# Gate and up of the 32 sample rows computed for two feed-forward steps at once, and the first down-projection operands requested earlier

## The reference

```python
def swiglu(h, w_gate, w_up, w_down):
    return (jax.nn.silu(h @ w_gate) * (h @ w_up)) @ w_down

yp = yp + swiglu(rms_norm(yp, g_ffn[l]), w_gate[l], w_up[l], w_down[l])
ys = ys + swiglu(rms_norm(ys, g_ffn[l]), w_gate[l], w_up[l], w_down[l])
```

## Time and profile before

| | |
|---|---|
| median of 3 runs | 1041.6 us (1041.6 to 1042.43) |
| the profiled execution | 1042.83 us, of which span 1041.1 us |
| PE busy | 1011.4 us, 97% of the span |
| DVE, ACT, POOL busy | 618.8, 390.7, 401.2 us |
| granted TensorE clock, mean | 0.994 of full |

### The profile page before, as it was taken

The page is one execution under the profiler, slowest core; times in us unless marked ns, Lnnn a source line. Parts: engine busy times, 40 slices in busy tenths (PEclk is TensorE's granted clock), DMA queues, the critical chain, the costliest instruction groups (busy, mean ns, idle before and its releaser), DMA issues.

```text
span 1041.1 us, 16425 instructions
## 1 busy us (share of the span) xinstructions
PE 1011.4 (97%) x5754; PEld 836.1 (80%) x5754; DVE 618.8 (59%) x918; ACT 390.7 (38%) x720; POOL 401.2 (39%) x445
## 2 busy tenths in 40 slices
PE   5999999999999999999999999999998999999996
PEld 4999998888887887887788787778877777877785
DVE  6375637756355686675575667666663737535725
ACT  6411245454232443333333333333333446334431
POOL 2010100000000457687696686776872300202055
PEclk9999999999999999999999999999999999999998
DMA  8311331101222444364554643643636999478814
GB/s 281 96 44 43 83 85 42 42 2 41 102 86 82 127 139 145 113 182 130 154 157 120 188 143 112 192 146 107 201 107 205 302 344 388 161 287 298 304 41 166
DMA packets 166658, 155.84 MB, mean 150 GB/s; under 512 B 16400, under 2 KB 129808, under 8 KB 166608
## 3 DMA queue, kind: packets, MB, share of 16 engines
q1 hardware_dynamic: 166608, 155.16, 46.4%
HBM read 114.17 MB, written 41.06 MB: 149 GB/s over the span
## 4 chain that ended last, share of the span: by engine, by line
PE 85%; DMA 6%; DVE 6%; ACT 1%; SPq 1%; issue 1%; POOL 1%; POOLq 0%; ACTq 0%; DVEq 0%
PE ps L1089 26%; PE ps L1090 25%; PE ps L1091 25%; DMA xd_in<-act_scratch 4%; PE ps L1371 2%; PE ps L1126 2%; DMA act_scratch<-act_sums 1%; PE ps L1261 1%; PE ps L1239 1%; DVE x_dn L1865 1%; DMA out_state_gmlp_v_sample<-work 1%; PE ps L1223 1%; DVE work L1950 1%; PE ps L1461 1%; DVE ln_st L1944 1%
## 5 line engine op out<-in xcount | busy, mean ns | idle before, releaser
L1089 PE MATMUL ps<-x_forms,w_forms 128*128 128x512 f32 (+1 forms) x644 | 248.4, 386 | 3.5 <-DVE w_forms L1865 2.5
L1090 PE MATMUL ps<-x_forms,w_forms 128*128 128x512 f32 (+1 forms) x644 | 245.9, 382 | 0.0
L1091 PE MATMUL ps<-x_forms,w_forms 128*128 128x512 f32 (+1 forms) x644 | 245.4, 381 | 0.0
L1089 PEld LDWEIGHTS ps<-x_forms,w_forms 128*128 128x128 f32 x644 | 121.8, 189 | 35.6 <-issue 8.3
L1091 PEld LDWEIGHTS ps<-x_forms,w_forms 128*128 128x128 f32 x644 | 121.8, 189 | 23.5
L1090 PEld LDWEIGHTS ps<-x_forms,w_forms 128*128 128x128 f32 x644 | 121.8, 189 | 22.3
L1089 PE MATMUL ps<-w_dn,x_dn 128*128 128x512 f32 x308 | 122.2, 397 | 3.3 <-DVE x_dn L1865 2.7
L1091 PE MATMUL ps<-w_dn,x_dn 128*128 128x512 f32 x308 | 120.7, 392 | 0.0
L1090 PE MATMUL ps<-w_dn,x_dn 128*128 128x512 f32 x308 | 120.5, 391 | 0.0
L941 POOL TENSOR_SCALAR meansq<-sumsq 128x1 f32<-128x1 f32 (+1 forms) x27 | 10.4, 385 | 255.0 <-ACT xn_ffn L1509 226.4
L1668 ACT CAST w_forms<-w_sums 128x512 fp32r<-128x512 f32 x88 | 54.6, 623 | 115.5 <-PE ps L1091 115.5
(11 more groups left out here) (246 smaller groups left out, 2094.4 us busy)
## 6 DMA issues: line engine op xcount, KB each, us to landing
xd_in<-act_scratch SPq DMA_DIRECT2D x35, 512.0 KB, 7.5
t_raw<-in_w_down SPq DMA_DIRECT2D x88, 128.0 KB, 2.6
act_scratch<-act_sums SPq DMA_DIRECT2D x22, 512.0 KB, 4.7
y_acc_odd<-in_w_down SPq DMA_DIRECT2D x22, 512.0 KB, 6.1
wd_in<-t_scratch SPq DMA_DIRECT2D x20, 512.0 KB, 7.5
wd_in<-in_w_down SPq DMA_DIRECT2D x15, 512.0 KB, 7.1
stage<-in_w_in SPq DMA_DIRECT2D x28, 256.0 KB, 3.7
w_stage_even<-in_w_gate SPq DMA_DIRECT2D x22, 256.0 KB, 3.4
```

The costliest lines, as they stand in the source:

```text
L1089: mm(out, wh, xh, start=first, stop=False, skip_group_check=onto)
L1090: mm(out, wh, xl, start=False, stop=False, skip_group_check=onto)
L1091: return mm(out, wl, xh, start=False, stop=last, skip_group_check=onto)
```

## The change

First, `sample_step(c, q)` becomes `sample_pair(c)`: the eight matmuls of both steps of a chunk stand together, after P2 of the second step of the chunk before, in one bank (columns 0 to 255 for the first step, 256 to 511 for the second). Copy, additions, SiLU, product and store each handle both halves at once, and are executed 11 times instead of 22. In the first step the pair stands after the first half `j = 0`. The waits follow: P6 waits for `sample_summed` only where `q == 1`, and `sample_pair` waits for the weights of both steps.

Second, SP asks for the first two weight operands of the down projection (`load_w(0)`, `load_w(1)`) before `store_step` of step 20, and for the first two activation operands before the last two pieces of down-weight sums. ACT and DVE take the first weight operand before `copy_p57` and `p5_p7` of the last step, and the first activation operand right behind them.

```diff
-            def store_sample(c, q):
-                sp.wait_ge(sample_hidden, 2 * c + (q + 1))
-                sp.dma_start(sample_scratch.ap()[:, bass.ds(2 * P * c + P * q, P)],
-                             sample_h[q][:, :]).then_inc(sample_out[q], 16)
+            def store_sample(c):
+
+                sp.wait_ge(sample_hidden, c + 1)
+                sp.dma_start(sample_scratch.ap()[:, bass.ds(2 * P * c, 2 * P)].rearrange("p (q t) -> p q t", q=2),
+                             sample_h[:, :, :]).then_inc(sample_out, 16)
...
             last = STEPS - 1
+            load_piece(CHUNKS - 1, 0)
+            store_sums(CHUNKS - 2)
+            store_piece(CHUNKS - 1, 0)
+            load_piece(CHUNKS - 1, 1)
+            store_piece(CHUNKS - 1, 1)
+            load_piece(CHUNKS - 1, 2)
             for i in range(2):
                 sp.wait_ge(y_spilled[i], 16 * len(range(i, ROWS, 2)))
+            load_w(0)
+            load_w(1)
+            store_step(CHUNKS - 1, 0)
+            load_x(0)
+            load_x(1)
+            store_piece(CHUNKS - 1, 2)
+            load_piece(CHUNKS - 1, 3)
             sp.wait_ge(hidden_out[0], 16 * CHUNKS)
-            for k in range(GROUPS_A_FORM):
+            for k in range(2, GROUPS_A_FORM):
                 load_w(k)
                 load_x(k)
...
-            def sample_step(c, q):
-
-                s = 2 * c + q
-                pe.wait_ge(w_landed[q], 64 * c + 64)
-                pe.wait_ge(u2_ready, s + 1)
-                if isinstance(s, int) and s == 0:
+            def sample_pair(c):
+
+                for q in range(2):
+                    pe.wait_ge(w_landed[q], 64 * c + 64)
+                pe.wait_ge(u2_ready, 2 * c + 1)
+                if isinstance(c, int) and c == 0:
                     pe.wait_ge(x_sample_ready, 1)
-                for k in range(KT):
-                    t = mm(ps[QUARTERS[k % 4], BANK_6[q], 0:2 * P].rearrange("p (h c) -> p h c", h=2),
-                           x_sample[:, k, :], w_stage[q][:, :, k, :], start=k < 4, stop=k >= KT - 4)
+                for q in range(2):
+                    for k in range(KT):
+                        out = ps[QUARTERS[k % 4], BANK_6[0], 2 * P * q:2 * P * q + 2 * P].rearrange("p (h c) -> p h c", h=2)
+                        t = mm(out, x_sample[:, k, :], w_stage[q][:, :, k, :], start=k < 4, stop=k >= KT - 4)
                 t.then_inc(sample_fed, 1)
...
             def ffn_step(c, q, more=True):
                 for p in range(PRODUCTS):
-                    product(2 * c + q, q, p)
-                    if p == P2 and more:
-                        sample_step(*((c, 1) if q == 0 else (c + 1, 0)))
+                    product(c, q, p)
+                    if p == P2 and q == 1 and more:
+                        sample_pair(c + 1)
...
             last = STEPS - 1
             copy_p1(last, 1)
+            down_weight_hi(0)
             copy_p57(last, 1)
-            form_hi(0, 0)
+            act_hi(0)
             silu_c11(last, 1)
...
             second_u(last, 1)
+            down_weight_lo(0)
             p5_p7(last, 1)
-            for g in range(3):
+            act_lo(0)
+            for g in range(1, 3):
                 form_lo(0, g)
```

More of the change, by code:

```diff
@@ L360, in build @@
         x_sample = place("x_sample", [P, KT, DEC], h_at + 63488)
-        sample_gu = [place(f"sample_gu{x}", [DEC, 2 * P], h_at + 64512 + 1024 * x) for x in range(2)]
-        sample_h = [place(f"sample_h{x}", [DEC, P], h_at + 66560 + 512 * x) for x in range(2)]
+        sample_gu = place("sample_gu", [DEC, 2, 2, P], h_at + 64512)
+        sample_h = place("sample_h", [DEC, 2, P], h_at + 66560)
         w_stage = [place("w_stage_even", [P, 2, KT, P], wbuf_at), place("w_stage_odd", [P, 2, KT, P], wbuf_at + 16384)]
@@ L509, in build @@
         sample_hidden = sem("sample_hidden")
-        sample_out = [sem(f"sample_out{x}") for x in range(2)]
+        sample_out = sem("sample_out")
         act_sum_1 = sem("act_sum_1")
@@ L791, in store_piece, with ffn_pair @@
                              t_out[x % 2][:, :, :]).then_inc(t_stored[x % 2], 16)
-            def ffn_pair(c, more):
-                if more:
-                    next_weights(2 * c, 0)
+            def ffn_pair(c):
+                next_weights(2 * c, 0)
                 load_piece(c, 0)
@@ L801, in ffn_pair @@
                 load_piece(c, 1)
-                if more:
-                    next_weights(2 * c + 1, 1)
+                next_weights(2 * c + 1, 1)
                 store_piece(c, 1)
@@ L806, in ffn_pair @@
                 if isinstance(c, int) and c == 0:
-                    store_sample(0, 0)
+                    store_sample(0)
                 store_step(c, 0)
-                store_sample(c, 1)
                 store_piece(c, 2)
                 load_piece(c, 3)
[L813 to L816, removed]
+                store_step(c, 1)
+                store_sample(c + 1)
+                store_piece(c, 3)
+            ffn_pair(0)
             with sp.Fori(1, CHUNKS - 1) as c:
[L818 to L822, removed]
+                ffn_pair(c)
             def load_w(k):
@@ L877, in _ @@
                 if k == 2:
-                    for x in range(2):
-                        sp.wait_ge(sample_out[x], 16 * CHUNKS)
+                    sp.wait_ge(sample_out, 16 * CHUNKS)
                     for x in range(4):
@@ L1702, in silu_c12, with first_quarter, silu_sample @@
                 nc.scalar.activation(cc[q][:, 1, cols], cc[q][:, 1, cols], ACT.Silu).then_inc(c12_silu, 1)
-            def first_quarter(c, q):
-                s = 2 * c + q
-                act.wait_ge(sample_fed, s + 1)
-                if not isinstance(s, int) or s >= 2:
-                    act.wait_ge(sample_hidden, s - 1)
-                nc.scalar.copy(sample_gu[q][:, :], ps[QUARTERS[0], BANK_6[q], 0:2 * P]).then_inc(sample_first, 1)
-            def silu_sample(c, q):
-                act.wait_ge(sample_summed, 2 * c + (q + 1))
-                nc.scalar.activation(sample_gu[q][:, 0:P], sample_gu[q][:, 0:P], ACT.Silu).then_inc(sample_silu, 1)
+            def first_quarter(c):
+                act.wait_ge(sample_fed, c + 1)
+                if not isinstance(c, int) or c >= 1:
+                    act.wait_ge(sample_hidden, c)
+                nc.scalar.copy(sample_gu[:, :, :, :].rearrange("p q h t -> p (q h t)"), ps[QUARTERS[0], BANK_6[0], :]
+                               ).then_inc(sample_first, 1)
+            def silu_sample(c):
+                act.wait_ge(sample_summed, c + 1)
+                nc.scalar.activation(sample_gu[:, :, 0, :], sample_gu[:, :, 0, :], ACT.Silu).then_inc(sample_silu, 1)
             for i in range(ROWS):
@@ L1749, in _ @@
             weight_hi(0, 1, 2)
-            silu_sample(0, 0)
+            silu_sample(0)
             copy_p57(0, 0, 1)
@@ L1756, in _ @@
             silu_c12(0, 0, 1)
-            first_quarter(0, 1)
             weight_hi(0, 1, 6)
-            silu_sample(0, 1)
             def ffn_step(c, q):
@@ L1774, in ffn_step @@
                 weight_hi(*following, 6)
-                silu_sample(*following)
+                if q == 1:
+                    silu_sample(c + 1)
             ffn_step(0, 1)
@@ L2279, in ffn_step @@
                 hidden(s, q)
-                hidden_sample(*following)
+                if q == 1:
+                    hidden_sample(c + 1)
             ffn_step(0, 1)
```

51 lines of the change are left out of this document (25 added, 26 removed).

## The result

The changed kernel takes **1035.24 us** (median of 4 runs, 1034.6 to 1036.26) against 1041.6 us: ratio 0.9939, 95% interval 0.9927 to 0.9951, 6.4 us less. A second comparison (`e8_after_again`) gave 0.9924 (0.9909 to 0.9939), 7.1 us less. The forecast was 1032.7 us, its range 1031.5 to 1036.5. The median is above the 1031.5 to 1034.2 us that the prediction gave to its own sum; it is inside the range because that reached on to partial forms of the rivals. The profiled execution took 1034.63 us where that of before took 1042.83 us, so the two traces differ by 8.2 us and the medians by 6.4: the execution of before was 1.2 us over its median and this one 0.6 us under. Nothing was predicted of the part before 348 us, and its end moved by 0.1 us between these two traces (first P1 at 350.97 and 350.88 us).

What follows compares the result with a forecast made beforehand. PE was taken to bound the feed-forward loop, with the DMA queue nearly full where the down projection begins. 3.6 + 1.0 + 3.8 + 0.5 = 8.9 us off the median 1041.6 gave 1032.7 us, range 1031.5 to 1036.5.

Steps and rivals of the forecast that it cites:

- Part 1: Pairs in the steady steps: one passage into and out of small tiles saved per pair, ten pairs, 3.6 us (2.8 to 4.0).
- I take 0.36: Passage saved per steady pair, in us, chosen from 0.28 to 0.40 because only the first wave took 0.24.
- Part 2: First pair: 1.24 us leaves the first step's end, extra work fills PE's wait, 0.2 us stall; 1.0 us (0.7 to 1.2).
- Part 3: Start of the down projection: wait 2.73 plus low clock 1.5 less a P3 stall of 0.4, 3.8 us (3.0 to 4.3).
- landing at 795.2: First weight load of the down projection lands midway between 794.25 and 796.05 us, so P3 stalls 0.4 us.
- The copy waits long: Rival at the last P3: `wd_in(0)` takes 7.4 us, P3 stalls 3.2 us, the clock falls; 1037.0 us, chance 0.12.
- an outcome without a stall: Before the last P3: followers take nothing from `wd_in(0)`, landing nearer 3.6 us, no stall, sum 0.4 us larger.
- The clock term: Start of the down projection: without the 2.73 us wait PE's clock doesn't fall, nine starts take 1.5 us less.
- Part 4: Sample additions in the down projection: queue gains about 5 us against PE's 3.8, the 0.6 us wait goes; 0.5 us (-3.8 to 0.6).
- ready some 5 us earlier: Third activation operand of the down projection, now behind two loads instead of in a queue of six; `blocks` and `hidden` follow.
- given back at the sample additions: Rival: the queue's chain doesn't move, PE waits 4.4 us there, parts 3 and 4 give nothing; 1037.0 us, chance 0.10.
- signs of being wrong: A PE wait over 1.5 us at P3 or the sample additions, or two steps still taking 40.6 us.

Runs made afterwards that it cites:

- e8_after_again: The changed kernel, unaltered, timed and traced a second time: 1034.26 us, 0.9924 of the kernel before.
- e7: The changed kernel with the pair's two halves apart, after P7 and after P2 of the same step, evacuated together: 1037.87 us, 0.9969 of the kernel before.
- e6: The changed kernel with only the first weight operand requested early; the second and both activation operands behind the last down-weight sums: 1037.68 us, 0.9963 of the kernel before.
- e3: The changed kernel with `copy_p57` ahead of the first weight cast on ACT and `p5_p7` ahead of the subtraction on DVE: 1033.61 us, 0.9921 of the kernel before.
- e1: The changed kernel with the tail of SP, ACT and DVE as before, so the pair alone: 1037.59 us, 0.9959 of the kernel before.
- f4: The kernel before, unaltered, run once more for a second trace: 1041.94 us in its one execution.
- e2: The kernel before with the changed tail of SP, ACT and DVE, so the early requests alone: 1039.24 us, 0.9975 of the kernel before.
- g2: The kernel of e3 run again: 1034.38 us, 0.9936 of the kernel before.
- f1: The changed kernel with the last step's `blocks`, `hidden` and SiLU ahead of the third operands on DVE and ACT: 1036.17 us, 0.9951 of the kernel before.
- g1: The kernel of f2 with SP's last store behind the fifth pair of loads and last sums ahead of two raw loads: 1031.17 us, 0.9901 of the kernel before.
- f2: The kernel of e3 with the last step's `blocks`, `hidden` and SiLU ahead of the third operands: 1035.99 us, 0.9944 of the kernel before.
- e4: The kernel of e3 with DVE's first sample additions two groups of operands earlier in its list: 1032.88 us, 0.9912 of the kernel before.

## Why the prediction was right, and where not

**Part 1 was right, its size too small.** The passage is there and belongs to the change of tiles, as e7 shows. The step that was mis-sized is "I take 0.36" from the starts of the waves: it measured 40.61 - 40.17 = 0.44 us a pair, 4.4 us instead of 3.6. The starts of the first three waves gave 0.21 to 0.24 us a wave; the two lengths of a step give 0.20: a group of four waves costs 20.31 - 84 x 0.227 = 1.24 us, one of eight 40.17 - 168 x 0.227 = 2.04 us, so four waves are 0.80 us and the passage is the other 0.44. The Trainium skill, "TensorEngine Tiling (Array Packing)", Key Properties, says that a change of the tiling mode drains TensorE. This case agrees in so far as each group of small tiles costs 0.44 us besides its waves. The combining operations with 512 columns cost nothing, as argued: PE has no wait from 391 to 753 us of the changed kernel's trace.

**Part 2 was right.** P6 starts at 367.12 instead of 367.21 us, so its wait had covered the longer pair. P3 came 0.2 us later (373.25), as forecast. It gave 0.74 instead of 1.0 us: the sample matmuls that went away had taken 1.09 us there and not 1.24, and from P6 to the second step PE lost 0.35 us and not 0.2.

**Part 3, three terms.** The wait of 2.73 us is gone, as said. The stall before P3 is 1.2 and not 0.4 us: the term "landing at 795.2", 4.55 us after its issue, was mis-sized; the load took 5.2 us, near the 5.4 of the upper bound. The reason for taking less, that the load stood closer behind the `t_raw` loads before, did not hold: it was issued 1.15 us after the first of the two (784.51 us), where before it was 1.22 us (794.83 and 796.05). And one reason given against the rival "The copy waits long" was wrong in itself: "this one has only 256 KB". It is a load of 512 KB, as the part on DMA issues of both pages has it (count, size, median us to landing; here after):

```profile
wd_in<-in_w_down SPq DMA_DIRECT2D x15, 512.0 KB, 6.5
```

From the rule of the Trainium skill, "DMA: Bandwidth & Descriptors", Queues, rings and completion order, that each engine consumes a ring's descriptors in order, the prediction had drawn an outcome without a stall. That outcome did not come, at 5.2 us; but whether the loads behind it had a part in these 5.2 us no run shows (4.5 us in e6 without them, 4.6 in e3 with them), so the rule itself is not tested here. The clock term gave 1.74 us between these two traces (at the 0.227 us a start of part 1 its own sum is 1.6, not 1.5), but its reason, that the clock's fall is tied to a wait of such length, did not hold: 2.6 us in e1 and 1.8 us in f4 were followed by a clock of 1.00. The fall belongs to one execution and not to the kernel.

**Part 4 is the step that failed.** It said that the queue gains 5 us against PE's 3.8 and that the wait for the additions goes away. DVE's additions moved by 8.3 us, of which 5.3 are parts 1 and 2, which move everything: the queue gained 3.0 us and not 5. The loss is at the term "ready some 5 us earlier" for the third activation operand. It was ready 8.5 us earlier (cast at 800.90 us, before 809.36), 3.1 us beyond parts 1 and 2, and `blocks` behind it came from 9.5 to 4.9 us behind P4's last matmul. SP may issue the third pair of loads only when the store of step 20 has landed. In the new order that store stands behind the first two weight loads (not behind all four loads, as the section on the change has it), and it took 6.1 us to land where it had taken 2.5. (Behind no such load it took 2.5 to 2.7 us in before, f4 and e1; behind one 4.7 us in e6; behind two 5.6 to 6.3 us in after, e8, e2, e3, g2, f1 and g1.) So the third activation load was issued only 0.6 us earlier beyond parts 1 and 2; what it gained is its own landing, 7.7 instead of 10.2 us. The chain of waits of the changed kernel has these pieces and those that follow, up to the additions:

```profile
786.67 6.12 DMA act_scratch<-ffn_blocks_even
...
793.22 7.66 DMA xd_in<-act_scratch
...
817.24 10.35 DMA act_scratch<-act_sums
...
832.23 9.55 DMA xd_in<-act_scratch
...
844.14 8.67 DMA xd_in<-act_scratch
...
855.17 9.84 DMA xd_in<-act_scratch
...
866.12 1.08 DVE x_dn L1874
...
868.54 0.60 DVE y_acc_sample L2336
```

Between the sums and the additions no piece of the chain is PE's: the store of the sums must land, SP then issues some loads, and three activation loads follow each other, each issued when the one ahead of it in the same staging place has been cast and subtracted. (In g2 the chain is on PE up to 828.7 us and runs over three such loads from there.) And the wait at the additions is no remainder that vanishes; it decides the end. Starts in us of the first P1 of the feed-forward steps, the last store of sums on SP, the additions on DVE, and PE's last matmul (the first P1 moves by up to 2.0 us between traces, before any changed place; the last column takes that out):

| Kernel | first P1 | sums issued | additions | last matmul | last - additions | last - first P1 |
|---|---|---|---|---|---|---|
| before | 350.97 | 825.67 | 876.77 | 1032.43 | 155.66 | 681.46 |
| f4 (before again) | 350.40 | 823.01 | 875.84 | 1031.58 | 155.74 | 681.18 |
| e2 requests only | 350.97 | 821.04 | 872.86 | 1028.55 | 155.69 | 677.58 |
| e7 pair split | 350.14 | 820.69 | 871.83 | 1027.49 | 155.66 | 677.35 |
| e6 one load early | 349.98 | 818.84 | 870.91 | 1026.57 | 155.66 | 676.59 |
| f2 | 351.30 | 818.84 | 870.48 | 1026.20 | 155.72 | 674.90 |
| e1 pair only | 349.87 | 818.84 | 870.20 | 1026.04 | 155.84 | 676.17 |
| f1 | 350.15 | 818.82 | 869.85 | 1025.54 | 155.69 | 675.39 |
| after | 350.88 | 816.72 | 868.46 | 1024.27 | 155.81 | 673.39 |
| e8 (after again) | 351.09 | 816.98 | 868.44 | 1024.11 | 155.67 | 673.02 |
| g2 | 349.54 | 816.22 | 868.31 | 1024.02 | 155.71 | 674.48 |
| e3 | 350.54 | 815.50 | 866.88 | 1022.53 | 155.65 | 671.99 |
| e4 additions early | 349.32 | 815.92 | 863.27 | 1022.75 | 159.48 | 673.43 |
| g1 store early | 351.24 | 812.81 | 862.41 | 1021.87 | 159.46 | 670.63 |

In twelve of the fourteen traces the last matmul starts 155.65 to 155.84 us after the additions, and these 51.0 to 52.8 us after the sums are issued, whatever PE waited for or not at P3 and at the start of the down projection. What PE wins there by itself it gives back, all or in part, at the additions or at the raw loads beside them: counted from the first P1, the kernel before with no fall of the clock (f4) was 2.6 us ahead at the 20th matmul, 0.4 us behind the additions and 0.3 us at the end. So the sum's two terms "2.73" and "1.5" were not the gain. The gain of part 3 is that the queue's chain moved by 3.0 us. It can be read a second way: from e1, which has parts 1 and 2 alone, to the changed kernel the last column falls by 2.8 and 3.2 us. In between SP works off a list of loads in a nearly full queue (1.05 of its time and 388 GB/s from 840 to 878 us in f4). Where the last store and the sums went earlier (g1, with early `blocks` and SP's own order changed), the additions moved with them, until PE alone set the end.

**The sum.** 8.9 us predicted, 8.2 us between the profiled executions, 6.4 us between the medians. Of the 1.8 us between the last two, 1.2 are that the execution of before was over its median and 0.6 that the other was under. The prediction carried its 8.9 us over to the median unchanged, though 2.73 and 1.5 us of it had been read in one execution (f4 has 1.8 us and none). That the range held is in part luck: parts 3 and 4 said 4.3 us and gave 2.6 (e2) to 3.0 us, in another way than described, and part 1 gave 0.8 us more than said. Of the rivals, "given back at the sample additions" describes the mechanism best, but not its size, since the chain did move. "The copy waits long" came true by 1.2 us, which e3 and g2 show to be worth nothing measurable. Of the signs of being wrong none came (waits of 1.2 and 0.8 us, two steps in 40.17 us), but the gap before P3 was twice the 0.6 us named.

**What stays open:** why e3 and g2, the same kernel, part by 2.4 us between the 20th matmul and the additions; what the clock's fall in one execution followed from; how much of the first load's 5.2 us is due to what stands behind it; why the store of the blocks takes longer to land in f1; and whether g1's order of SP gains anything without the early `blocks`.

## What to carry to other kernels

Where PE waits at several places of a stretch and the data of the last wait come by a chain without PE, that last one sets the end: before a gap or a slow clock ahead of it is counted as a gain, write down when the data for that last wait would come, and what instruction starts them. Where SP issues every DMA from one list, data that are ready early gain nothing (f1) until their store stands early in that list (g1), and a store that is moved behind big loads lands late (6.1 instead of 2.5 us here). When traces are compared, count from a place ahead of the change: here that place alone moved by 2.0 us. Matmuls on small tiles among full ones are best put together: each further group of eight cost 0.44 us here, besides its own matmuls.

## What was not expected of the hardware

- The clock: 0.58 behind a wait of 2.73 us in one trace, 1.00 behind waits of 2.6 us (e1) and 1.8 us (f4) at the same place. It also differs between traces where nothing was changed, behind the start of the first step (PE had waited 2.50 us ahead of it in the one and 1.85 us in the other); the stretch before, then after:

```profile
352.00:354.00 2.00, 2.00 (x13) 2.00 (x12) 1.16 (x2) 1.41 (x3) 0.10 (x1) 0.59 0.30 123
```

```profile
352.00:354.00 2.00, 2.00 (x19) 2.00 (x18) 1.07 (x2) 1.50 (x3) 0.19 (x1) 1.00 0.35 143
```

- The first load of a weight operand, 512 KB, took 5.2 to 5.6 us in eight traces and 4.6 us in a ninth, all with three such loads and a store issued within some 3 us behind it, and 4.5 us with the store alone (e6). The store of 256 KB behind it took 6.12 us, and 2.5 us before the change; the third activation operand took 7.66 us.
